# Six of eight experts taken in order of their row counts, the two smallest with 64 slots, and the first up tiles loaded into the down ring

## What is computed

```python
logits = (t @ w_router).astype(F32)                 # t: 256 x 1024
top_v, top_i = lax.top_k(logits, TOP_K)             # TOP_K = 2
wts = jax.nn.softmax(top_v, axis=-1)
gate = jnp.sum(jax.nn.one_hot(top_i, N_EXPERTS, dtype=F32) * wts[..., None], axis=1)
for e in range(N_EXPERTS):                          # 8 experts, width 3584
    ye = swiglu(t, w_gate[e], w_up[e], w_down[e]).astype(F32)
    out = out + gate[:, e:e + 1] * ye
```

## Time and profile before

| what | before |
|---|---|
| median of 3 runs | 1663.01 us (1662.38 to 1663.93) |
| the profiled execution | 1663.85 us, of which the span 1662.1 us |
| TensorE busy | 1642.2 us (99%) |
| bytes moved by DMA | 487.59 MB, mean 293 GB/s |
| chain that ended last | TensorE 87%, VectorE 9% |

### The profile page before, as it was taken

How to read it: one execution, slowest core, us unless ns; L and a number is a source line. 1 busy time by engine, 2 the same in 40 slices (tenths; PEclk the granted TensorE clock), 3 DMA queues, 4 the chain that set the end, 5 groups by cost and what they waited for, 6 DMA issues and landing times.

```text
span 1662.1 us, 29811 instructions
## 1 busy us (share of the span) xinstructions
PE 1642.2 (99%) x13234; PEld 928.0 (56%) x13234; DVE 657.3 (40%) x930; ACT 507.7 (31%) x961; POOL 144.6 (9%) x209
## 2 busy tenths in 40 slices
PE   9999999999999999999999999999999999999998
PEld 7777888888888888887333333333333333333332
DVE  8998547667656975574000102002001020020011
ACT  7878564654446775552000000000000000000000
POOL 5251000123000400001000000000000000000000
PEclk9999999999999999998999999999999999999999
DMA  7444334755535444357999999999999999999994
GB/s 251 153 153 149 131 127 157 242 197 183 178 133 170 154 152 144 112 195 292 424 423 414 412 417 422 413 415 414 414 423 400 419 407 411 415 401 421 419 398 181
DMA packets 142558, 487.59 MB, mean 293 GB/s; under 512 B 10172, under 2 KB 34872, under 8 KB 142424
## 3 DMA queue, kind: packets, MB, share of 16 engines
q1 hardware_dynamic: 138920, 474.07, 73.8%
q0 software_dynamic: 3408, 11.54, 2.5%
q10 hardware_dynamic: 96, 0.02, 0.0%
HBM read 478.64 MB, written 6.95 MB: 292 GB/s over the span
## 4 chain that ended last, share of the span: by engine, by line
PE 87%; DVE 9%; issue 1%; ACT 1%; DMA 0%; SPq 0%; DVEq 0%; ACTq 0%
PE ps L1502 35%; PE ps L1538 17%; PE ps L898 10%; PE ps L900 10%; PE ps L899 10%; DVE ring_lo L2355 3%; PE ps L1175 1%; PE ps L891 1%; DVE turned L2613 1%; PE ps L1147 1%; DVE z L2571 1%; PE ps L1158 1%; ACT hi_m L1712 0%; DVE costab L2490 0%; PE ps L1481 0%
## 5 line engine op out<-in xcount | busy, mean ns | idle before, releaser
L1502 PE MATMUL ps<-ring_h,xe 128*32 128x448 f32 x5376 | 511.3, 539 | 0.0
L1502 PEld LDWEIGHTS ps<-ring_h,xe 128*32 128x32 f32 x5376 | 173.4, 110 | 327.3 <-issue 325.8
L1538 PE MATMUL ps<-ring_d,aT 128*32 128x512 f32 x2520 | 276.0, 592 | 0.0
L2984 DVE TENSOR_TENSOR acts<-ps,gates 128x1344 f32<-128x1344 f32 x16 | 24.9, 1558 | 628.6 <-PE ps L1502 628.6
L2355 DVE TENSOR_TENSOR ring_lo<-ring,hi_m 128x1024 fp32r<-128x1024 f32 x160 | 190.2, 1230 | 31.8 <-ACT hi_m L1712 31.3
L900 PE MATMUL ps<-hi_m,xT_lo 128*128 128x512 f32 (+1 forms) x528 | 202.6, 384 | 0.0
L1712 ACT ACTIVATE hi_m<-ring 128x1024 fp32r<-128x1024 f32 x160 | 160.7, 1055 | 115.7 <-PE ps L900 112.4
L1538 PEld LDWEIGHTS ps<-ring_d,aT 128*32 128x32 f32 x2520 | 81.5, 110 | 183.4 <-issue 183.3
L898 PE MATMUL ps<-hi_m,in_hi 128*128 128x512 f32 (+1 forms) x416 | 164.2, 395 | 4.9 <-DVE ring_lo L2355 3.7
L899 PE MATMUL ps<-ring_lo,in_hi 128*128 128x512 f32 (+1 forms) x416 | 158.8, 382 | 0.0
L2216 ACT ACTIVATE xe<-ps 128x384 f32<-128x384 f32 x12 | 5.9, 491 | 424.5 <-PE ps L1481 424.5
(11 more groups left out here) (437 smaller groups left out, 1781.7 us busy)
## 6 DMA issues: line engine op xcount, KB each, us to landing
ring_d<-in_moe_w_down SPq DMA_DIRECT2D x112, 1024.0 KB, 19.2
ring_h<-in_moe_w_gate SPq DMA_DIRECT2D x112, 896.0 KB, 15.6
ring_h<-in_moe_w_up SPq DMA_DIRECT2D x112, 896.0 KB, 13.4
ring<-in_w_in SPq DMA_DIRECT2D x50, 1024.0 KB, 5.1
hT<-in_moe_w_gate SPq DMA_DIRECT2D x16, 896.0 KB
hT<-in_moe_w_up SPq DMA_DIRECT2D x16, 896.0 KB
ring<-in_ffn_w_gate SPq DMA_DIRECT2D x22, 512.0 KB, 3.9
ring<-in_ffn_w_up SPq DMA_DIRECT2D x22, 512.0 KB, 4.9
```

Source lines behind the costliest of these rows:

```text
L1502: last = nc.tensor.matmul(ps[GROUP * i:GROUP * (i + 1), banks + g, 0:BLOCK].rearrange("p (b j) -> p b j", j=GROUP), xe[:, k, own + GROUP * ...
L1538: last = nc.tensor.matmul(ps[GROUP * q:GROUP * (q + 1), 4 + half, :], activations(h)[:, 2 * i + odd, GROUP * g:GROUP * (g + 1)], w[:, odd, ...
L2984: V.tensor_tensor(acts[:], ps[:, bank:bank + 3, 0:BLOCK], gates[:], ALU.mult).then_inc(sem("products_ready"), 1)
```

## The change

Experts 0 and 1 stay first (`FIXED = 2`). The other six are taken in descending order of their row counts; VectorE computes the order (`expert_order`, in place of `busiest_expert`), and permutes slots and gates by it (`slot_at`, `gate_at`). The last two places (`SHORT = 2`) get 64 slots, two groups of 32: 8 matmuls for a tile in place of 12. From half 4 on SP reads the expert numbers into registers (`load_order`) and computes the source address of each load with them. The check for the further passes now also asks that the two last have at most 64 rows.

The first seven up tiles of half 0 go into the seven places of `ring_d` and are issued before half 0 starts; all later hidden tiles move on by seven places in the ring of eight.

```diff
+    FIXED, SHORT = 2, 2
+    SORTED = NE - FIXED
+        def hidden_place(n):
+            if KD <= n < KD + RD:
+                r = (n - KD + 2) % RD
+                return ring_d[:, r, 0:WIDE], (full_d[r], 16 * EARLIER[r])
+            m = n if n < KD else n - RD
+            return hidden_tile(m % RH), (full_h[m % RH], 16 * (m // RH + 1))
+        SHORT_ROUNDS = tuple(tuple((odd, half, g) for half in range(2) for g in range(2)) for odd in range(2))
+        def groups(e):
+            return 3 if e < NE - SHORT else 2
...
+            def load_order():
+                sp.wait_ge(sem("routed"), 1)
+                for i in range(SORTED):
+                    experts_at.append(sp.value_load(order_i[0:1, i:i + 1], min_val=0, max_val=NE - 1))
-            def load_hidden(n, w, e, half, k):
-                if n >= RH:
-                    sp.wait_ge(sem("hidden_tiles_used"), n - RH + 1)
+            def load_hidden(n):
+                if n >= KD + RD:
+                    before_ = n - RD - RH
+                    sp.wait_ge(sem("hidden_tiles_used"), before_ + 1 + (0 if before_ < KD else RD))
                 elif n == RH - 1:
                     sp.wait_ge(sem("logits_done"), 1)
+                elif n == KD:
+                    sp.wait_ge(sem("merged_ready"), 2 * L)
+                    sp.wait_ge(sem("mixer_hi_ready"), 2 * L * MIX_TILES)
+                elif n == KD + RD - 2:
+                    sp.wait_ge(sem("columns_done"), COL_TILES * L)
...
+            FIRST_LOADS = (*range(KD - 1), *range(KD, KD + RD - 2), KD - 1, *range(KD + RD - 2, 2 * KD))
             for t in range(HALVES):
+                if t == 2 * FIXED:
+                    load_order()
+                for n in FIRST_LOADS if t == 0 else range(2 * KD * t, 2 * KD * t + KD):
+                    load_hidden(n)
                 if t >= 1:
                     load_downs(t - 1, 0)
+                    for n in range(2 * KD * t + KD, 2 * KD * (t + 1)):
+                        load_hidden(n)
                     load_downs(t - 1, 1)
...
-                        pool.indirect_dma_start(taken[0:CAP], None, rows, row_index(e + 1)).then_inc(sem("rows_taken"), 16)
+                        pool.indirect_dma_start(taken[0:slots(e + 1)], None, rows, row_index(e + 1)).then_inc(sem("rows_taken"), 16)
...
-                        for g in range(3):
+                        for g in range(groups(e)):
...
-                        for round_ in DOWN_ROUNDS:
+                        for round_ in down_rounds(e):
...
                 def first_pass():
                     dispatch(0)
                     normed_rows_low(1)
-                    busiest_expert()
                     for half in range(2):
                         scale_gathered(0, half, 6 - 2 * half)
-                    route_weights()
...
                     last.then_inc(sem("rows_normed"), 1)
-                    ramps_of_last()
+                    expert_order()
+                    route_weights()
```

More of the change, by code:

```diff
@@ L268, in decoder_trunk @@
         most = fb("most", [P, 1], I32)
-        last_ramps = fb("last_ramps", [P, 2, P])
+        counts = fb("counts", [P, NE])
+        place = fb("place", [P, SORTED])
+        at_place = fb("at_place", [P, SORTED, SORTED])
+        order = fb("order", [P, SORTED])
+        order_i = fb("order_i", [P, SORTED], I32)
+        slot_at = fb("slot_at", [P, C, NE])
+        gate_at = fb("gate_at", [P, C, NE])
+        spill = fb("spill", [P, NE])
         ffn.close()
@@ L302, in taken_blocks, with slots, last_rows_of @@
             return range(part * KT, (part + 1) * KT)
+        def groups(e):
+            return 3 if e < NE - SHORT else 2
+        def slots(e):
+            return GROUP * groups(e)
+        def last_rows_of(half):
+            return slice(2 * GROUP * half, 2 * GROUP * (half + 1))
         def rows_at(h):
@@ L834, in expert_rows, with slot_indices @@
                 pool.dma_start(sums[SEQ:SEQ + P], x[:, 0, :]).then_inc(sem("rows_stored"), 16)
-                def slots(pair):
+                def slot_indices(pair):
                     pool.wait_ge(sem("slot_values_taken"), pair + 1)
@@ L2914, in route, with expert_order, by_place @@
                                              in1=sel[:].bitcast(F32), op0=ALU.add, op1=ALU.mult))
-            def busiest_expert():
+            def expert_order():
+                others = slice(FIXED, NE)
                 dve.wait_ge(sem("places_done"), 1)
-                chain(V.tensor_reduce(rstat[:, 4:5], ps[:, 3, 2 * NE:3 * NE], AX.X, ALU.max))
+                chain(V.tensor_copy(counts[:], ps[:, 3, 2 * NE:3 * NE]))
+                mine, other = spread(counts[:, others], 2, SORTED), spread(counts[:, others], 1, SORTED)
+                same, more = (cmp_[:, i, 0, 0:SORTED, 0:SORTED] for i in (1, 0))
+                V.tensor_tensor(same, other, mine, ALU.is_equal)
+                chain(V.tensor_tensor(more, other, mine, ALU.is_gt))
+                chain(V.tensor_tensor(same, same, tie[:, 0:SORTED, 0:SORTED], ALU.mult))
+                chain(V.tensor_tensor(more, more, same, ALU.add))
+                chain(V.tensor_reduce(place[:], more, AX.X, ALU.add))
+                chain(V.tensor_tensor(at_place[:], spread(place[:], 1, SORTED), spread(ramp[:, 0:SORTED], 2, SORTED),
+                                      ALU.is_equal))
+                def by_place(dst, values):
+                    chain(V.tensor_tensor(same, at_place[:], spread(values, 1, SORTED), ALU.mult))
+                    chain(V.tensor_reduce(dst, same, AX.X, ALU.add))
+                by_place(order[:], ramp[:, others])
+                chain(V.tensor_copy(order_i[:], order[:]))
+                by_place(order[:], counts[:, others])
+                V.tensor_scalar(order[:, SORTED - SHORT:SORTED], order[:, SORTED - SHORT:SORTED], float(GROUP), None, ALU.add)
+                chain(V.tensor_reduce(rstat[:, 4:5], counts[:], AX.X, ALU.max))
+                chain(V.tensor_reduce(rstat[:, 6:7], order[:, SORTED - SHORT:SORTED], AX.X, ALU.max))
+                chain(V.tensor_tensor(rstat[:, 4:5], rstat[:, 4:5], rstat[:, 6:7], ALU.max))
@@ L2920, in busiest_expert @@
                 V.tensor_copy(most[:], rstat[:, 4:5]).then_inc(sem("routed"), 1)
                 V.memset(rstat[:, 5:6], 0.0).then_inc(sem("added"), 1)
+                V.memset(spill[:], float(CAP))
+                chain(V.tensor_copy(slot_at[:, :, 0:FIXED], slot_of[:, :, 0:FIXED]))
+                V.tensor_scalar(spill[:, others], place[:], float(SORTED - SHORT), -float(GROUP), ALU.is_ge, ALU.mult)
+                for c in range(C):
+                    by_place(slot_at[:, c, others], slot_of[:, c, others])
@@ new lines, in expert_order, with gates_by_place @@
+                chain(V.tensor_scalar(spill[:, others], spill[:, others], float(CAP), None, ALU.add))
+            def gates_by_place():
+                others = slice(FIXED, NE)
+                same = cmp_[:, 1, 0, 0:SORTED, 0:SORTED]
+                chain(V.tensor_copy(gate_at[:, :, 0:FIXED], gate[:, :, 0:FIXED]))
+                for c in range(C):
+                    chain(V.tensor_tensor(same, at_place[:], spread(gate[:, c, others], 1, SORTED), ALU.mult))
+                    chain(V.tensor_reduce(gate_at[:, c, others], same, AX.X, ALU.add))
```

122 lines of the change are left out of this document (72 added, 50 removed).

## The result

| what | before | changed |
|---|---|---|
| median | 1662.72 us (1662.38 to 1663.93, 4 runs) | 1646.21 us (1644.32 to 1648.34, 4 runs) |
| ratio | | 0.9897, 95% interval 0.9885 to 0.991 |
| profiled execution, its span | 1663.85, 1662.1 us | 1648.34, 1646.6 us |

1645.5 us was predicted. A second set of the changed kernel gave 1645.84 us (1645.2 to 1648.33), ratio 0.9898. The profile shown here is of the slowest of the eight executions, so its times at the end lie some 2 us above the median's.

What follows compares the result with a forecast made beforehand. TensorE bounds the kernel, the DMA right behind. Last landing 1640.1 - 3.0 - 1.6 - 2.3 = 1633.2, last product 1635.0, with the 9.6 us tail a span of 1644.6, median 1645.5 us; range 1637 to 1655.

Steps and rivals of the forecast that it cites:

- The bound: Experts' halves: TensorE bounds by some 0.3 us a half, the DMA full right behind; cutting TensorE's work makes DMA the bound.
- the rival where TensorE alone bounds: All experts: TensorE's 72 us saved count in full, 1591 us, needing 611 GB/s; no separate chance given.
- Last landing, last tile, tail: Kernel's end: last landing 1633.2, then 0.1 and 1.7 us to the last down product at 1635.0, tail 9.6 us.
- The DMA's own idle end: Last loads: idle time waiting for TensorE to free places goes, gaining 3 us (2 to 4).
- The lead: Around half 0: early up tiles fill 15.2 us, a new DMA stop costs 12.9; net 2.3 us (0 to 5).
- SP's registers: Loads from half 4 on: register loads and address arithmetic cost zero; at worst some 2 us of DMA idling.
- one of my own signs of being wrong: Short halves at the end: a DMA share under 1 while TensorE waits would prove the prediction wrong.
- a possible lead of 6 us more: Loads: lead can grow from 12.3 us to an empty queue's 6.3; rival of more lead, 1638 us, chance 0.07.
- VectorE's added work: Routing before half 0: 28 small chained operations, 6 to 9 us, in a gap where VectorE otherwise waits.
- Row traffic: Short experts' gathers and scatter: a third of one scatter and two gathers saves 1.6 us (0.5 to 2.5).
- TensorE's waits: Last four halves: from between 1440 and 1470 TensorE waits for DMA, 50 to 60 us in total.
- The slower rival: Starved last halves: granted clock stays below 0.69, TensorE binds again, about 1710 us; clock chance 0.04.

Runs made afterwards that it cites:

- Experiments 1: Changed kernel with only the last expert at 64 slots, the seventh at 96 again; 1648.17 us, ratio 0.9909.
- experiment 2: Changed kernel with all eight experts at 64 slots, tokens beyond the 64th of an expert left out; 1629.42 us, ratio 0.9797.
- experiment 5: Changed kernel run again unaltered, as common base for the runs beside it; 1645.84 us.
- experiment 6: Changed kernel with half 0's seven down tiles issued ahead of the eighth gate tile of half 1; 1645.33 us against 1645.84 beside it.
- experiment 10: Changed kernel with four experts in place of two at 64 slots, without early down tiles; 1639.62 us, ratio 0.9857.
- experiment 7: Changed kernel with half 0's down tiles issued early and four experts in place of two at 64 slots; 1643.47 us.
- Experiment 8: All eight experts at 64 slots, and each of seven scatters writing only its first 32 rows; 1628.95 us against 1629.42 with full scatters.
- experiment 11: All eight experts at 64 slots, and six of eight hidden tiles of each product given 4 matmuls for 8; 1626.21 us.

## Why the prediction was right, point by point

**The bound.** Right. The loads stood right behind TensorE, at 54.4 us a half against 54.7, and took over as soon as matmuls went. Experiments 1 and 2 show it from both sides: half the short experts keep 14.7 of 16.5 us of gain, four times as many give twice as much (33.5). With all of them short, the first gate tiles of half 3 and half 15 land at 900.3 and 1544.2, 53.7 us a half. That is the loads' own pace with 64 rows for each gather and scatter. So in the short halves TensorE's pace had 1.0 us to give, more than the 0.3 us that I read between 54.7 and 54.4; the sum doesn't use this 0.3. Two small slips change nothing either: slice 38 has 398 GB/s, not 400 or more, and the rival where TensorE alone bounds needs 608 GB/s (22.02 MB in 36.2 us), not 611.

**Last landing, last tile, tail.** The sum had the last down product end at 1635.0. In experiment 5, whose execution lies next to the median, the last tile starts at 1632.71 and takes 1.92 us: 1634.6. The tail is 9.6 us there and in the profiled execution, as in the sum. The profiled execution shown above ends 2.3 us later. Its loads moved 384 GB/s from 1200 to 1250 where experiment 6 and the run with four short experts have 417, a slow spell of some 4 us that no part of the change explains. That the forecast came within 0.7 us of the median is in part luck: the last landing gained 7.4 us in experiment 5 (1640.1 to 1632.7) where the sum has 6.9, but its terms are off one by one, as the next two points show. By the landings of first gate tiles 3.5 us of the 7.4 are there at half 12 (1404.4 before, 1400.9), 4.8 at half 15 (1565.9, 1561.1), and the rest comes after it.

**The DMA's own idle end.** Half right. The idle time of before is gone: the share is 1.02 from 1600 to 1627, and the last issue comes at 1619.8, 15.2 us before landing, where it was at 1633.8 with 6.3. But a new idle end stands in its place: a share of 0.49 from 1627 to 1634 (3.6 us idle), and in experiment 5 one of 0.45 from 1628 to 1633 (2.8 us). Before, it was 3.3 us (shares of 0.61 from 1624 to 1628 and 0.13 from 1638 to 1640). By idle time little of the 3 us of this term was won. The new idle end is also one of my own signs of being wrong, a share under 1 while TensorE waits. TensorE's last four tiles still start 2.35 to 2.49 us apart there, the pace of a full DMA, with 202 GB/s moving. That would fit some of the 16 DMA engines being done early while the others carry the rest at their full rate; the trace gives only the mean of the 16, so this is not shown. The same end is there in the other profiles whose loads are the bound for long: 229 GB/s from 1620 to 1626 in experiment 10, 222 from 1606 to 1614 in experiment 2.

**The lead.** The fill and the stop came where I had them, but each was smaller than I counted. Before, the shares of rows 2 leave 9.9 us idle from 760 to 780, not 15.2, so that 5 us of the seven tiles were still queued at 778 when I took the queue to be empty. The work on hand then lasted to about 805, not 799.4, and the stop cost 6.2 us by the share of 0.48 in 12 us, not 12.9. The difference is 3.7 us, where I had 2.3 net. The first gate tile of half 2 lands 14.3 us after its issue, 3.9 less than before, where I gave 2 to 3. It lands at 854.0, and at 859.0 before, 5.0 us sooner, of which TensorE's earlier start in this execution (774.70 against 775.80 for the first hidden matmul) is 1.1: 4 us. At the end 1.3 to 3.2 us are left. Both are within the bounds, but one more step of my reasoning failed: I took the 6.3 us of the last load as the landing of an empty queue, and so a possible lead of 6 us more. In experiment 5 landings of the first gate tile sink from 14.0 us at half 2 to 10.0 and 10.6 at halves 11 and 12, before the loads become the bound, and in experiment 7 they are at 10.3 to 11.2 from half 3 to half 7. The gate loads of half 11 in experiment 5 and of half 5 in experiment 7:

```profile
L649 SPq DMA_DIRECT2D ring_h<-in_moe_w_gate x1: 345/345/345, 1335.6 to 1335.6; - x1
DMA to landing us min/median/max: 10.0/10.0/10.0
...
L649 SPq DMA_DIRECT2D ring_h<-in_moe_w_gate x1: 355/355/355, 1005.7 to 1005.7; - x1
DMA to landing us min/median/max: 10.3/10.3/10.3
```

Four down tiles are issued right ahead of this tile (4 x 2.48 us), so that some 10 us should be its floor with the places full. By this count the lead had 4 us of room, not 6, and the changed kernel had used it before its loads became the bound. That fits experiment 6, where filling the stop gave nothing.

**SP's registers.** Zero was right. The register loads at half 4 don't show: gate tiles of half 4 are issued from 949.42, 54.9 us after those of half 3. Address arithmetic is 0.08 us for a load: on SP's own queue one FUSED_REGOPS of 46 ns and one MOVE of 29 ns stand before the DMA.

**VectorE's added work.** The order and the gates together are 37 operations, 28 of them new, and take 7.0 us from 778.34 to 785.4, at 0.06 to 0.20 us each, in a gap that was free to 811. ScalarE's first silu waited for the stored rows until 798.32 in place of 796.41; it ended at 800.9 and had 10 us to spare.

**Row traffic.** I priced a scatter at 3 us for 96 rows. Experiment 8 doesn't settle it. In the sum it is one scatter's third, 1 us at most.

**TensorE's waits.** 41.7 us, where 50 to 60 were expected: a starved tile shows 1.71 us of busy time for 1.50 us of work, since with nothing behind it the last matmuls' ends are counted too. For 70 waits that is 15 us, which makes up the difference. The first wait comes at 1446.7, within the 1440 to 1470 that I gave.

**The clock.** My claim that no wait is longer than part of a tile was wrong. After the scatter that GpSimd issued at 1465.3 TensorE waited 2.54 us, and the clock fell once: granted 0.83 and 0.75 in the two stretches of 4 us from 1472. It cost nothing: the tile then took 2.92 us, and by 1481.6 TensorE waited for a load again. The Trainium skill's rule ("TensorE: Matmul & The Clock Gate", section "HAM oscillation"), that waits for DMA between bursts bring the clock down, thus agrees in kind with the trace. The kernel of that section waits longer than it works, so that my "by that rule 1711" took more from the Trainium skill than it states. Here, with two thirds of the matmuls left, the clock does not fall at every burst: by stretches of 20 us from 800 to 1600 it is under 1.00 in one of 40, both in the changed kernel (0.91 from 1460) and in experiment 2 (0.91 from 1560). In experiment 11, with a third of the matmuls in most tiles, it is 0.77 to 0.89 by stretches of 50 us. The slower rival needed it to stay below 0.69, and no run came there.

## What to carry to other kernels

When two resources are within a few per cent of each other, cutting one gains only the slack of the other. Here most of it was the 12.4 us by which the last load landed ahead of TensorE's end. Take the last landing that the loads allow, and add one tile and the tail. For a gap that early loads are to fill, count its idle time and not the length of the loads. A lead won by early loads lasts only as far as the ring has places; compare a landing with the landing of the same tile in a full ring, not with that of a lone load. An edit that does nothing alone (the up tiles in the down ring, ratio 0.9999) can be worth some 2 us once another one has moved the bound.

## What the runs showed of the hardware that I had not expected

The DMA share stays at 1.01 to 1.02 whether the kernel is bound by the loads (415 to 424 GB/s by stretches of 50 us from 1450 to 1600 in the changed kernel) or by the places that TensorE frees (406 to 412 GB/s in experiment 6, by stretches of 100 us from 900 to 1400), so that a share of 1 doesn't prove that the DMA is the bound. Nor does a late landing: 18.2 us at half 2 of the kernel before, where TensorE never waits for a load. TensorE's waits do. And where the loads are the bound, the last 4 to 8 us of them run at about half the share in the profiles named above, with tiles still landing at full pace; why is open. At least two of the profiles have one stretch of 50 us at 383 or 384 GB/s, some 4 us of loads each, at different places; what causes them is open. TensorE, busy for 453 of 588 us in experiment 2 and waiting a little at most tiles, was granted 1.00 over that stretch.
